# Key drains ahead of convolutions, two-tensor operations as scalar-tensor-tensor, and fourteen selection half rounds between the index sums

## What is computed

```python
h = rms_norm(x, norm_g)
proj = h @ w_in                                   # 1024 x 7260
# A: sparse attention. An index score chooses 128 keys for each query
score = einsum('bqh,bqhs->bqs', w_idx, relu(q_idx @ k_idx)); sel = top_k(score, 128)
o_a = softmax(q k[sel] / 8 + bias) v[sel]
# B: gated DeltaNet on 64-token chunks
qkv = silu(causal_conv(b_qkv)); q, k = l2norm(q), l2norm(k)
beta = sigmoid(b_in); g = -exp(a_log) * softplus(a_in + dt_bias); g_cum = cumsum(g)
a = tril(beta k k^T * decay, -1); t_inv = inverse(I + a)      # then a scan over the chunks
# C: compressed, selected and window attention, three gates
kc = rms_norm(silu(blocks @ phi1) @ phi2)         # 31 compressed keys
x + (gA*(y_a@w_a) + gB*(y_b@w_b) + gC*(y_c@w_c)) @ w_out
```

## Time and profile before

| | us |
|---|---|
| median of 3 runs | 597.84 |
| lowest and highest | 596.25, 597.97 |
| the profiled execution | 597.7 |
| its span in the trace | 595.8 |
| PE busy | 545.4 (92%) |
| DVE, ACT, POOL busy | 390.1, 322.1, 221.1 |

### The profile page before, as it was taken

One profiled execution on the slowest core, in us unless ns is written; L12 is line 12 of the kernel. 1 busy time (PEld: TensorE's weight loads), 2 busy tenths in 40 slices (PEclk: granted clock), 3 DMA queues, 4 the chain that ended last, 5 costly groups with the idle time before them and its releaser, 6 DMA issues.

```text
span 595.8 us, 10710 instructions
## 1 busy us (share of the span) xinstructions
PE 545.4 (92%) x4087; PEld 308.0 (52%) x4087; DVE 390.1 (65%) x920; ACT 322.1 (54%) x573; POOL 221.1 (37%) x164
## 2 busy tenths in 40 slices
PE   2999999999999866999899998989899898999997
PEld 1644556543357532467466575645455465444443
DVE  6520388765498696876877768668797556687211
ACT  4555645355467962560922805586676768246320
POOL 0154453613046660352632630441321375154420
PEclk9999999999999996999999999999999999999999
DMA  9345865653124230220220210212211221172411
GB/s 316 114 125 137 167 96 162 189 164 89 56 54 125 75 107 33 72 72 2 73 72 2 64 45 2 59 49 72 72 36 38 70 72 37 36 282 72 142 53 54
DMA packets 31173, 52.93 MB, mean 89 GB/s; under 512 B 2743, under 2 KB 13329, under 8 KB 31121
## 3 DMA queue, kind: packets, MB, share of 16 engines
q1 hardware_dynamic: 30825, 51.68, 29.9%
q10 hardware_dynamic: 296, 0.55, 0.5%
HBM read 49.80 MB, written 2.42 MB: 88 GB/s over the span
## 4 chain that ended last, share of the span: by engine, by line
PE 68%; DVE 17%; ACT 7%; issue 5%; SPq 2%; DMA 1%; POOL 0%; DVEq 0%; ACTq 0%; PEldq 0%; POOLq 0%
PE bank L1690 13%; PE bank L1692 12%; PE bank L1691 12%; PE bank L1986 5%; PE bank L1988 5%; PE bank L1896 5%; PE bank L1990 5%; PE bank L1888 3%; PE bank L1726 3%; ACT stage L744 2%; PE bank L1832 2%; DVE bank L1266 1%; DVE early L1300 1%; DVE small L1297 1%; ACT late L966 1%
## 5 line engine op out<-in xcount | busy, mean ns | idle before, releaser
L532 POOL TENSOR_TENSOR w_lo<-stage,w_hi 128x1024 f16<-128x1024 f32 (+4 forms) x76 | 149.4, 1970 | 218.9 <-ACT w_hi L752 218.8
L752 ACT ACTIVATE w_hi<-stage 128x1024 f16<-128x1024 f32 (+4 forms) x76 | 74.5, 981 | 13.9 <-PE bank L1692 9.0
L1986 PE MATMUL bank<-hT_hi,w_hi 128*128 128x512 f16 x192 | 73.0, 380 | 1.7 <-PE bank L1990 0.9
L744 ACT ACTIVATE stage<-stage,small 128x512 f32<-128x512 f32 (+4 forms) x120 | 73.6, 663 | 0.7 <-DMA stage<-in_w_in 0.6
L1988 PE MATMUL bank<-hT_lo,w_hi 128*128 128x512 f16 x192 | 72.9, 380 | 0.3
L1990 PE MATMUL bank<-hT_hi,w_lo 128*128 128x512 f16 x192 | 72.8, 379 | 0.3
L1690 PE MATMUL bank<-w_hi,hT_hi 128*128 128x260 f16 (+4 forms) x192 | 61.4, 320 | 3.0 <-DVE hT_lo L1074 1.4
L1691 PE MATMUL bank<-w_lo,hT_hi 128*128 128x260 f16 (+4 forms) x192 | 61.0, 318 | 0.0
L1692 PE MATMUL bank<-w_hi,hT_lo 128*128 128x260 f16 (+4 forms) x192 | 61.0, 318 | 0.0
L1690 PE MATMUL bank<-hT_hi,w_hi 128*128 128x512 f16 (+1 forms) x128 | 48.0, 375 | 2.5 <-ACT work L735 1.4
L1691 PE MATMUL bank<-hT_lo,w_hi 128*128 128x512 f16 (+1 forms) x128 | 47.8, 373 | 0.0
(11 more groups left out here) (331 smaller groups left out, 1145.9 us busy)
## 6 DMA issues: line engine op xcount, KB each, us to landing
stage<-in_w_in SPq DMA_DIRECT2D x40, 512.0 KB, 3.6
stage<-in_c_phi_w SPq DMA_DIRECT2D x8, 512.0 KB, 4.1
stage<-in_w_branch SPq DMA_DIRECT2D x8, 512.0 KB, 3.8
stage<-in_w_out SPq DMA_DIRECT2D x8, 512.0 KB, 4.7
stage<-in_w_in SPq DMA_DIRECT2D x8, 260.0 KB, 2.8
strips<-rel_rows SPq DMA_DIRECT2D x8, 256.0 KB, 6.5
late<-in_x SPq DMA_DIRECT2D x1, 2048.0 KB, 9.1
out_x<-late SPq DMA_DIRECT2D x8, 256.0 KB, 2.0
```

What stands on the lines that cost most here:

```text
L532: gp.tensor_tensor(piece_view(w_lo[:, k % PAIRS, :], c), piece_view(stage[:, piece_at[c, j] % STAGES, :], c), piece_view(w_hi[:, k % PAIRS ...
L744: ins = nc.scalar.activation(full[:, r, :], full[:, r, :], ACT.Copy, scale=g_w[:, 2 * j + r:2 * j + r + 1])
L752: nc.scalar.activation(piece_view(w_hi[:, k % PAIRS, :], c), full, ACT.Copy).then_inc(hi_ready, 1)
L1986: mm(G.bank(g)[:, :], w[0], h[0], start=k == 0, stop=False)
```

## The change

Six edits, told by engine.

- **PE and its ring.** `kcT` moves ahead of `kk` in the ring. The two sums of the log decay follow `sqT` after B4's third tile, `cumulative(0)` follows B4's last tile, `kcT` goes to the first tile of B2, the key products behind that tile, and the transpose `n` to the second tile.
- **ScalarE.** `hi_split(CH_B2, 0)` moves from behind the gates to ahead of `silu_conv(7)`.
- **GpSimd.** The diagonal masks move earlier; the resets of the inverse stand ahead of `cumulative_input(0)`; the copies into `cmp_strip` stand behind the masked decays and B2's followers.
- **DVE, form.** `pair_op` replaces 25 `tensor_tensor` calls (many in helpers and loops) on two SBUF tensors by `scalar_tensor_tensor` with a factor of 1.0. The copy of `rk` becomes a maximum of a tensor with itself.
- **DVE, sums.** The three outputs from `sums` are made from PSUM instead of from a copy of it in SBUF.
- **DVE, order.** `compressed_keys` moves behind the log decays. `key_scales` stands ahead of `difference(0)`, `kcT` is taken out right behind it, and the part that needs the exponentials is `decay_scales`. Fourteen half rounds stand between the index sums, with two small work buffers of their own for the first seven rounds, and convolution 11 is the filler of the first inverse level.

```diff
-ROUNDS_IN, ROUNDS_LOG, ROUNDS_SUM, ROUNDS_ROOT, ROUNDS_CONV = 0, 1, 1, 1, (6, 4, 3)
+ROUNDS_FIRST = 14
+ROUNDS_IN, ROUNDS_LOG, ROUNDS_CONV = 0, 2, (3, 2, 2)
...
-        v_names += [("gc", 0), ("kk", 0), ("qk", 0), "kcT", ("n", 0)]
+        v_names += [("gc", 0), "kcT", ("kk", 0), ("qk", 0), ("n", 0)]
...
+            hi_split(CH_B2, 0)
             silu_conv(7)
...
-            hi_split(CH_B2, 0)
             drain(("B4", 1), raw_b[:, 1, 260:520], 260, scale=1.0 / W_SCALE)
...
+            def pair_op(out, a, b, op):
+                return ve.scalar_tensor_tensor(out, a, 1.0, b, ALU.mult, op)
...
-                    hold(ve.tensor_tensor(w, y, y, ALU.mult))
-                    hold(ve.tensor_tensor(w, w, ss, ALU.mult))
+                    hold(pair_op(w, y, y, ALU.mult))
+                    hold(pair_op(w, w, ss, ALU.mult))
...
             index_scores(4)
+            rounds(1)
             a_key(2)
+            rounds(2)
             index_scores(5)
+            rounds(2)
             index_scores(6)
             a_key(3)
-            for n in range(7, 12):
-                index_scores(n)
+            index_scores(7)
+            rounds(1)
+            index_scores(8)
+            rounds(2)
+            index_scores(9)
+            rounds(4)
+            index_scores(10)
+            rounds(2)
+            index_scores(11)
...
             for m in range(8):
+                if m == 7:
+                    rounds(2)
                 conv(m)
...
             ve.nop().then_inc(GATE_IN.sem, 1)
-            compressed_keys()
             rounds(ROUNDS_LOG)
...
             ve.nop().then_inc(gsum_ready, 1)
-            rounds(ROUNDS_SUM)
-            rounds(ROUNDS_ROOT)
+            compressed_keys()
...
-            ve.tensor_copy(sums_sb, ps[:, 0:32]).then_inc(v_drained, 1)
+            hold(ve.tensor_copy(gc_, ps[:, 0:16]))
+            ve.tensor_copy(gl_, ps[:, 16:32])
+            ve.tensor_tensor(kd_s, ps[:, 16:32], gc_, ALU.subtract).then_inc(v_drained, 1)
             ve.wait_ge(v_drained, V.filled("sums"))
-            ve.tensor_copy(gc_, sums_sb[:, 0:16])
-            ve.tensor_copy(gl_, sums_sb[:, 16:32])
-            hold(ve.tensor_tensor(kd_s, sums_sb[:, 16:32], sums_sb[:, 0:16], ALU.subtract))
...
+            key_scales()
             difference(0)
-            key_scales()
+            twin("kcT", kcT[:, 0, 0:N_CMP], kcT[:, 1, 0:N_CMP], R_CK, N_CMP)
+            decay_scales()
+            rounds(4)
+            conv(8)
+            decayed_products(0)
             rounds(ROUNDS_CONV[0])
-            conv(8)
+            level_zero(0)
             rounds(ROUNDS_CONV[1])
             conv(9)
-            decayed_products(0)
-            twin("kcT", kcT[:, 0, 0:N_CMP], kcT[:, 1, 0:N_CMP], R_CK, N_CMP)
             rounds(ROUNDS_CONV[2])
-            level_zero(0)
             conv(10)
-            conv(11)
...
+                    if (c, l, late_in_level) == (0, 1, False):
+                        conv(11)
+                        return
...
             def between_b2(t):
-                if t == 1:
+                if t == 0:
                     key_products(0)
 
             def within_b2(t, k):
                 if (t, k) == (0, 2):
-                    cumulative(0)
-                if (t, k) == (2, 1):
                     T_IN.wait(pe, "kc")
                     transposes("kcT", [raw_c0[0:N_CMP, 0, 0:128]], N_CMP)
-                if (t, k) == (3, 1):
+                if (t, k) == (1, 6):
                     GD.wait(pe, ("nnt", 0))
```

More of the change, by code:

```diff
@@ L231, in trunk @@
         topk_work = [early[:, 5120:5632], early[:, 5632:6144]]
+        topk_first = [late[:, 3840 + 256 * n:4096 + 256 * n] for n in range(2)]
         relu_buf = [late[:, 640:1152], late[:, 1152:1664], late[:, 2176:2688], early[:, 2048:2560]]
@@ L563, in _, with mask_diagonal @@
                 follow(CH_QI, t)
+            def mask_diagonal(q):
+                gp.wait_ge(score_ready, q)
+                d = scores[q - 1][:, P * q:P * q + P]
+                gp.affine_select(out=d, in_=d, compare_op=ALU.is_ge, fill=NEG, base=0, pattern=[[-1, P]],
+                                 channel_multiplier=1).then_inc(diag_ready, 1)
             for c in (CH_A2, CH_B0):
@@ L623, in _ @@
             reset(t_hT)
+            cumulative_input(0)
             for t in range(1, 4):
                 follow(CH_B4, t)
+            masked_decays(0)
+            follow(CH_B2, 0)
+            follow(CH_B2, 1)
+            follow(CH_B2, 2)
             gp.wait_ge(strips_loaded, 16 * (P // ROW_COPIES))
@@ L1117, in _ @@
             y, w = inv_root("C0", ss_c, 20, 1.0 / 64)
-            hold(ve.tensor_tensor(ss_c, y, w, ALU.mult))
+            hold(pair_op(ss_c, y, w, ALU.mult))
             ssc = ss_c.rearrange("p (t g) -> p t g", t=NT)
@@ L1129, in _ @@
             y, w = inv_root("C1", ss_w, 4, 1.0 / 64)
-            hold(ve.tensor_tensor(ss_w, y, w, ALU.mult))
+            hold(pair_op(ss_w, y, w, ALU.mult))
             for s in range(2):
@@ L1214, in _ @@
             y, w = newton_root("Ak", ss_k, 16)
-            hold(ve.tensor_tensor(ss_k, y, w, ALU.mult))
+            hold(pair_op(ss_k, y, w, ALU.mult))
             for a in range(2):
@@ L1240, in a_key, with topk, rounds @@
                 twin(("ak", h), k_a[:, h, 0, :], k_a[:, h, 1, :], R_AK)
+            def topk(q):
+                ve.wait_ge(diag_ready, q)
+                src = scores[q - 1]
+                for r in range(TOPK // 8):
+                    m8 = max8[:, 8 * (r % 2):8 * (r % 2) + 8]
+                    hold(ve.max(m8, src))
+                    yield
+                    dst = (topk_first if q == 1 and r < ROUNDS_FIRST // 2 else topk_work)[r % 2][:, 0:P * (q + 1)]
+                    hold(ve.match_replace(dst, m8, src, TAKEN))
+                    src = dst
+                    if r < TOPK // 8 - 1:
+                        yield
+                hold(ve.tensor_scalar(src, src, TAKEN, -NEG, ALU.is_equal, ALU.mult))
+                ve.tensor_scalar(keep_add[q - 1], src, NEG, None, ALU.add).then_inc(keep_ready, 1)
+                yield
+            topk_steps = chain(topk(1), topk(2), topk(3))
+            def rounds(n):
+                for _ in range(n):
+                    next(topk_steps, None)
             index_scores(0)
@@ L1449, in compressed_softmax @@
                 hold(ve.tensor_scalar(crq[:, 0, :], crq[:, 0, :], seen[:, 0:1], None, ALU.mult))
-                hold(ve.tensor_tensor(crq, crq, gate[:, :, :, 0], ALU.mult))
+                hold(pair_op(crq, crq, gate[:, :, :, 0], ALU.mult))
                 yield
@@ L1568, in finish @@
                 if m != "A":
-                    hold(ve.tensor_tensor(fac, fac, gate[:, q, :, 1 if m == "sel" else 2], ALU.mult))
+                    hold(pair_op(fac, fac, gate[:, q, :, 1 if m == "sel" else 2], ALU.mult))
                 ve.wait_ge(o_filled, O.filled(("o", m, q)))
```

78 lines of the change are left out of this document (26 added, 52 removed).

## The result

The changed kernel takes 592.13 us (median of 4 executions, 591.14 to 592.99), beside 597.30 of the kernel before in the same comparison: a ratio of 0.9912, interval 0.9891 to 0.9933. The profiled execution took 591.1 us with a span of 589.3; that of before was 597.7. The forecast was 588.5 in 582.5 to 593.5: the direction and the range hold, but of the 9.3 us forecast 5.2 came.

The account below looks back on a forecast made before the run. PE was taken as nearly always full except for waits, chiefly 9.65 us at kcT, and half clock after it. The profiled 597.7 - 7.5 - 2.0 + 0.5 gave 588.7, rounded to 588.5 us, range 582.5 to 593.5.

Parts of the forecast that it names:

- The hole goes, a new wait takes its place: PE between B4 and B2: the 9.65 us wait at kcT goes, a 6.5 us wait ahead of cumulative(0) comes.
- The 1.74 us at `sqT`: PE's smaller hole at 199.26 us, ended by ScalarE's line 905; goes with the earlier weight split.
- the half rounds between the index sums: Fourteen on DVE while it waits for ScalarE: hidden; up to 6.6 us if that cover were gone.
- Scalar-tensor-tensor buys nothing: Some eighty DVE operations change form; the new form waits for GpSimd as the old does: no gain, no loss.
- Rivals A and B: A: one-column operations slip past GpSimd, 584.5, chance 0.15. B: the new form is not held at all, 580.5, 0.09.
- The clock: PE after the wait at cumulative(0): first matmuls at half speed, 2.0 us charged (0 to 4).
- Small gaps: PE and DVE finish B2 about level near 232 us: 0.8 us charged.
- the inverse: Rounds inside the inverse get wider sooner: +0.5 us (0 to 1.5).
- the stretch: From B4's third tile's last matmul to the second inverse level: 49.4 us falls to 41.9, -7.5.
- Of the 3.6 us that PE lost I give back -2.0: Attention units: eleven fewer half rounds left there, at some 0.75 us each; -2.0 us (0 to -3).
- Rival C: Gain half given back: wait 7.5, clock costs 4, attention phase yields nothing; 593.5 us, chance 0.14.
- the larger of the prediction's own two bounds, 594.5: The whole kernel's time in us with the small bounds all on one side; the other bound is 585.

Follow-up runs that it names:

- root_psum: The changed kernel with the inverse roots' work values in the idle PSUM bank of convolution 6, three small copies added to each root: 587.64 us, ratio 0.9840.
- form_back: The changed kernel with all its two-tensor operations written as tensor-tensor again: 592.21 us, ratio 0.9909 to the kernel before.
- rounds_back: no_copy with eleven of the fourteen half rounds taken out of the index sums, back where the kernel before had them: 588.97 us, ratio 0.9858.
- before_no_copy: The kernel before without the 128x256 copy that starts each selected group's sum, nothing else changed: 595.88 us, ratio 0.9973.
- no_copy: The changed kernel without the 128x256 copy that starts each selected group's sum; the sums read the compressed output directly: 588.27 us, ratio 0.9847.
- scales_first: root_psum_no_copy with sqT's copy, sums, key scales and difference(0) ahead of the compressed keys; PE takes kcT, key products and n later: 585.89 us.
- root_psum_no_copy: The changed kernel with both the roots' work values in PSUM and no 128x256 copy in the selected groups: 585.60 us, ratio 0.9795.
- keys_early_psum: keys_early with the roots' work values in PSUM besides: 583.81 us, ratio 0.9763 to the kernel before.
- keys_early: no_copy with compressed_keys moved back ahead of the log decays, and two half rounds moved behind decay_scales: 585.61 us, ratio 0.9800.

## Why the prediction was right, and where it was off

- **The hole goes, a new wait takes its place: right, to 0.3 us.** It was put at 6.5 us ahead of `cumulative(0)`, ended by the copy of `sqT`; it is 6.80, ended by L1356. The mechanism is shown by root_psum: the same products with one operand in PSUM are not held, and PE's wait halves. The 1.74 us at `sqT` went and the half rounds between the index sums cost nothing, both as forecast.
- **Scalar-tensor-tensor buys nothing: right**, shown by form_back (592.21 for 592.13). The page of the Trainium skill (SBUF — State Buffer, Who interferes with whom) that the prediction named holds for one column too: 2.18 us for two products. Of an instruction with at most one input in SBUF, outside the modes that use both ports, the same section of the Trainium skill says that it does not contend; root_psum's products agree with 0.17 us each beside a split. Rivals A and B are out: of A's operations of one column only a scalar one slipped past a split.
- **The clock: 2.45 for 2.0.** It fell 4.9 us after PE stopped (4.3 before) and came back 4.9 us after PE resumed: 0.98 more in `cumulative(0)` and 1.5 in the first seven matmuls of B2.
- **Small gaps 0.9 for 0.8, the inverse +0.4 for +0.5: right.** With the above the stretch gave -6.7 for -7.5.
- **The step that failed: "Of the 3.6 us that PE lost I give back -2.0" in the attention units.** It measured 0.0 in the profiled execution. The half rounds did what was forecast of them: about 2 us there between the two profiles, 1.5 in rounds_back. But the sum had no term for the copy of L1578, which the trace of before shows 0.01 us ahead of a split, on the path of PE's next unit. The forecast moved the half rounds, and with them the one that stands just ahead of this copy; the copy came 0.05 us behind the split and took the 2 us back. In medians the copy costs the kernel before 2.2 us and the changed one 3.9 (before_no_copy, no_copy), so 1.7 us of the gain went there.
- **The sum on medians.** Without the copy on both sides the change gives 7.6 us, where 9.3 were forecast. With it, it gives 5.2 in the first comparison and 5.8 by form_back's set (598.03 to 592.21). The medians of the kernel before differ by as much between the sets (597.27 to 598.04).
- **Rival C** (593.5: the gain half given back) is nearest to the median, by luck. Its wait of 7.5 and its clock cost of 4 did not come. Its third part did, an attention phase that yields nothing, but by the copy, which it did not have.
- **The range** of 582.5 to 593.5 does not take in the larger of the prediction's own two bounds, 594.5, though the prediction says that it does.

## What to carry to other kernels

When an edit puts a chain of small VectorE operations into a time in which GpSimd runs long ones, count the chain by GpSimd's boundaries and not by its own durations; a work tensor in an idle PSUM bank took the products of such a chain out of that queue here. Before a stretch is promised to the end, look in the later stages for pairs that are hundredths of a microsecond apart, a copy and a split here: a half round of another kind, 0.06 us longer, turned this pair round, and the price was the whole split, and probably clock on top in most executions. A short copy on the way to PE's next unit costs its own time even where nothing holds it. And a late step that is moved out of one wait has to be followed to the next point that needs it: scales_first lost behind B2 more than it had won inside it.

## What was not expected of the hardware

- Behind the same wait of PE, 2.17 us, the granted clock was 0.5 for 3.4 us in root_psum (400 to 405) and stayed up in the profiled execution of the changed kernel. Waits of 3.53 and 3.54 us at one place brought it down once and once not. In before_no_copy it was 0.72 from 365 to 370, right behind waits of 0.90 and 0.37 at 362.04 and 362.98; the kernel before has the same two waits (363.61, 364.55) and 1.00 there. What a wait costs beyond itself is thus uncertain here, between nothing and about the 2.45 us of the changed kernel; the misses of 0.6 and 0.3 us in root_psum_no_copy and keys_early_psum would fit that.
- Two SBUF tensors are not the only operations that were held. With one SBUF tensor each, the copy of 128x256 (2.23 us, 0.29 alone), the key copies of 31x64 (1.92 for two that take 0.41) and scalar operations of 128x32 were; a scalar operation of 31x1 was not.
- GpSimd's splits in a row, without a pause between them, let one VectorE operation through at each boundary: 1.83, 2.06 and 2.05 us for three scalar operations of 32 columns that take 0.18 alone (keys_early).
